# An encoder layer on one core: attention queues from a planner, output kept turned, next head's loads on GpSimd

## The reference

```
h = rms(x, g_pre_mix);  z = h @ w_in  -> q, k, v, forget logits, B, C, u
attn[t] = softmax_{s<=t}( q_t.k_s/8 + sum_{s<j<=t} logsigmoid(f_j + b_f) ) @ v     8 heads of 64
conv    = B * causal_conv3(C * u)                                                 512 channels
mix = concat(rms(attn, g_attn_out), rms(conv, g_conv_out)) @ w_o
x = x + rms(mix, g_post_mix)
x = x + rms(relu(rms(x, g_pre_mlp) @ w_up)^2 @ w_down, g_post_mlp)
```

## Time and profile before

| | us |
|---|---|
| median of 3 runs (2731.07 to 2736.04) | 2732.44 |
| the profiled execution, its own time | 2737.44 |
| its span, first to last instruction | 2735.8 |
| input projection, to the first score matmul | 621.9 |
| attention, to the first mixing product | 462.6 |
| mixing, to the MLP's block | 223.9 |
| MLP | 1427.4 |

### The profile page before, as it was taken

How to read it: one execution, slowest core, us unless ns; L and a number is a source line. 1 busy time by engine, 2 the same in 40 slices (tenths; PEclk the granted TensorE clock), 3 DMA queues, 4 the chain that set the end, 5 groups by cost and what they waited for, 6 DMA issues and landing times.

```text
span 2735.8 us, 41595 instructions
## 1 busy us (share of the span) xinstructions
PE 2664.9 (97%) x14966; PEld 2405.3 (88%) x14966; DVE 1515.6 (55%) x2603; ACT 1126.6 (41%) x2099; POOL 1300.7 (48%) x884
## 2 busy tenths in 40 slices
PE   8999999998999999999999999899999999999997
PEld 8999999897888888888889989889999988999996
DVE  5233344247888887765344344665556564556554
ACT  3201301107777877555333332534333344333433
POOL 3233334220101006553477776766556677566654
PEclk9999999999999999999999999999999999999999
DMA  6643534574565443568444546421211272212213
GB/s 199 199 123 110 175 108 142 189 199 103 124 150 122 100 102 117 167 183 244 143 168 163 196 169 225 170 74 64 77 61 61 85 277 96 73 61 66 72 61 108
DMA packets 294353, 364.26 MB, mean 133 GB/s; under 512 B 37576, under 2 KB 245392, under 8 KB 290128
## 3 DMA queue, kind: packets, MB, share of 16 engines
q1 hardware_dynamic: 257152, 316.15, 37.7%
q0 software_dynamic: 11808, 26.74, 3.1%
q10 hardware_dynamic: 25264, 19.66, 2.1%
HBM read 264.30 MB, written 97.94 MB: 132 GB/s over the span
## 4 chain that ended last, share of the span: by engine, by line
PE 46%; DVE 2%; POOL 1%; DMA 1%; issue 1%; ACT 0%; SPq 0%; DVEq 0%; POOLq 0%; ACTq 0%
PE dn_bank L3006 17%; PE up_bank L2982 15%; PE dn_bank L2962 7%; PE up_bank L2937 7%; DMA m_raw_up<-in_w_up 1%; DVE m_raw_up L2758 1%; POOL m_y L2517 1%; POOL m_w_up L2466 1%; DVE m_t L2758 0%; SPq L2342 0%; ACT m_junk L2659 0%; DVE m_y L2863 0%; DMA m_x<-scratch_x 0%; POOL m_u L2509 0%; DVE m_y L2817 0%
## 5 line engine op out<-in xcount | busy, mean ns | idle before, releaser
L3006 PE MATMUL dn_bank<-m_w_dn,m_u 128*128 128x512 f32 x2304 | 531.0, 391 | 5.4 <-ACT m_y L2692 4.3
L3006 PEld LDWEIGHTS dn_bank<-m_w_dn,m_u 128*128 128x128 f32 x2304 | 432.7, 188 | 96.0 <-ACT m_y L2692 4.0
L2982 PE MATMUL up_bank<-m_h,m_w_up 128*128 128x384 f32 x2688 | 476.1, 337 | 8.7 <-DVE m_stage L2772 4.5
L2982 PEld LDWEIGHTS up_bank<-m_h,m_w_up 128*128 128x128 f32 x2688 | 470.1, 189 | 12.7 <-issue 5.1
L2819 DVE TENSOR_TENSOR m_y<-dn_bank,m_y 128x1024 f32<-128x1024 f32 x168 | 205.7, 1224 | 270.4 <-PE dn_bank L3006 270.4
L508 POOL TENSOR_TENSOR w_lo<-w_raw,w_hi 128x1024 fp32r<-128x1024 f32 x72 | 176.0, 2448 | 342.3 <-DVE w_hi L722 342.3
L2509 POOL TENSOR_TENSOR m_u<-m_stage,m_u 128x384 fp32r<-128x384 f32 x128 | 141.5, 1128 | 281.7 <-ACT m_u L2648 281.7
L2466 POOL TENSOR_TENSOR m_w_up<-m_raw_up,m_w_up 128x512 fp32r<-128x512 f32 x128 | 192.2, 1521 | 65.2 <-ACT m_w_up L2616 65.2
L938 PE MATMUL proj<-ha_hi,w_hi 128*128 128x384 f32 (+1 forms) x640 | 212.1, 331 | 0.0
L1446 DVE TENSOR_TENSOR p_lo<-t_bank,p_hi 128x512 fp32r<-128x512 f32 (+1 forms) x336 | 197.9, 599 | 25.2 <-ACT p_hi L1393 24.6
L938 PE MATMUL proj<-ha_hi,w_lo 128*128 128x384 f32 (+1 forms) x640 | 210.0, 328 | 0.0
(11 more groups left out here) (304 smaller groups left out, 5674.4 us busy)
## 6 DMA issues: line engine op xcount, KB each, us to landing
m_raw_up<-in_w_up SPq DMA_DIRECT2D x48, 1024.0 KB, 5.4
m_raw_dn<-in_w_down SPq DMA_DIRECT2D x47, 1024.0 KB, 4.9
w_raw<-in_w_in SPq DMA_DIRECT2D x72, 512.0 KB, 4.1
scratch_h_pairs<-m_pieces POOLq DMA_DIRECT2D x12, 1792.0 KB, 8.2
m_h<-scratch_h_pairs SPq DMA_DIRECT2D x14, 1536.0 KB, 10.8
nck<-scratch_ncum SPq DMA_DIRECT2D x8, 1312.0 KB, 19.2
scratch_v_hl<-vhl SPq DMA_DIRECT2D x20, 512.0 KB, 2.7
q_hi<-scratch_q_hi SPq DMA_DIRECT2D x16, 528.0 KB, 7.3
```

Source lines behind the costliest of these rows:

```text
L2982: mm = pe.matmul(out, w_up[:, j, wp, k, :], hidden_rows(g, j, hp, k), start=(k == 0 and p == 0), stop=(k == KH - 1 and p == 2))
L3006: mm = pe.matmul(bank[:, cols], part, wd[:, wp, b, cols], start=(b == 0 and p == 0), stop=(b == 1 and p == len(passes) - 1))
```

## The change

- The looped order becomes one list of groups for all eight heads (attention_steps), in the order 0, EXTRA, 1, 2, 3. attention_order walks through it like a small planner: it has a cost and a latency for each step on PE, DVE and ACT, and appends to the engine's queue the step that can start first, by FIRST_CHOICE on a tie.
- N is gone. o_bank stays turned: ScalarE copies its lower and its upper 64 partitions to two places of o_t, GpSimd adds and scales them with 64 partitions and 512 columns, SP stores to attn_t (columns by rows). There are two o_bank.
- The scales are needed along columns now: VectorE makes a group's reciprocals at its first T, SP stores them to the scratch tensor rtotal and loads them back broadcast to 64 partitions.
- GpSimd issues the ten loads of head h+2 after it has closed group 3 of head h, and in the place of those of head 8 the eight of w_o. SP has the stores and the scales.
- g_attn_out and g_conv_out are multiplied into w_o by GpSimd, ahead of each split. The mixing loads attention rows turned from attn_t: its transposes and the multiplications by the gains are gone. Both squares and their sums are on GpSimd (sum_blocks), both rests too (rests), both high parts on ScalarE (firsts). A second matmul sums the attention's squares.

```diff
-S_BANKS, T_BANKS, O_BANKS = 3, 3, 1
-DELAY = {"act": {"M": 6, "T": 1, "O": 3, "N": 2}, "dve": {"M": 1, "T": 3}}
+S_BANKS, T_BANKS, O_BANKS = 3, 3, 2
 P_BUFS = 4
-A_BUFS = 5
+A_BUFS = 2
+GROUP_ORDER = (0, EXTRA, 1, 2, 3)
+SPLITS = {0: (5, 6), EXTRA: (4,), 1: (7, 0, 1), 2: (2, 3)}
+FIRST_CHOICE = {"pe": "TSV", "dve": "TS", "act": "TMO"}
...
+    def cost(engine, x):
+        if engine == "pe":
+            if x.kind == "S":
+                return 2 * (x.width / 2.4 + 13) + (107 if x.last else 0), 320
+            if x.kind == "T":
+                return 109 * (x.width // P), 260
+            return (2 * len(x.blocks) * 107 if x.group.extra else 2 * (x.width / 2.4 + 13)), 300
+        if engine == "dve":
+            return x.width / 0.96 + 67, 150
+        if x.kind == "O":
+            return 2 * (x.width / 1.2 + 150), 50
+        return x.width / 1.2 + (285 if x.kind == "M" else 125), 100
...
+    while True:
+        chosen = None
+        for engine, kinds in FIRST_CHOICE.items():
+            for rank, kind in enumerate(kinds):
+                n = taken[engine][kind]
+                if n < len(flat[kind]):
+                    x = flat[kind][n]
+                    start = max(free[engine], ready(engine, x))
+                    if start < math.inf and (chosen is None or start < chosen[0] or (start == chosen[0] and engine == chosen[1] and rank < chosen[2])):
+                        chosen = start, engine, rank, x
...
@@ sync @@
+            for q in groups:
+                store_scales(q)
+                load_scales(q)
+                if q is final[3]:
+                    sp.wait_ge(taken, S_BANKS + ALL_TAKEN)
+                    stored(final[0])
+                    stored(final[EXTRA])
                     front.load_first(sp)
+                if q.k:
+                    store(groups[q.k - 1])
...
@@ gpsimd @@
+            def fetch(head):
+                par = head % 2
+                pool.wait_ge(blank, 2)
+                if head >= 2:
+                    pool.wait_ge(used, P_BUFS + groups[GROUPS_OF * (head - 1) - 1].products[-1].at + 1)
+                if head == HEADS:
+                    front.load_weights(pool)
+                    return
+                load_queries_keys(pool, dr, head, q_hi[par], q_lo[par], k_hl[par], qk_fetched[par])
+                load_decay(pool, dr, head, nck[par], nck_fetched[par])
+                load_values(pool, dr, head, v_hl[par], v_fetched[par])
+
+            def close(q):
+                place, halves = att[0:HD, q.k % A_BUFS, 0:wide(q)], [o_t[0:HD, q.k % 2, i, 0:wide(q)] for i in range(2)]
+                pool.wait_ge(o_taken, O_BANKS + q.k + 1)
+                if q.k >= A_BUFS:
+                    pool.wait_ge(att_stored[q.k % A_BUFS], 16 * (q.k // A_BUFS))
+                pool.tensor_tensor(place, halves[0], halves[1], ALU.add).then_inc(added, 1)
+                pool.wait_ge(added, q.k + 1)
+                pool.wait_ge(scales_loaded[q.k % 2], 16 * (q.k // 2 + 1))
+                pool.tensor_tensor(place, place, scales[0:HD, q.k % 2, 0:wide(q)], ALU.mult).then_inc(att_done, 1)
+
+            fetch(1)
+            for q in groups:
+                if q is final[3]:
+                    pool.wait_ge(taken, S_BANKS + ALL_TAKEN)
                     front.set_ones(pool)
+                    front.sum_blocks(pool, 0, 0)
+                    front.rests(pool, 0, 0)
+                close(q)
+                if q.head == HEADS - 1 and q.g in SPLITS:
+                    for k in SPLITS[q.g]:
+                        front.split_weights(pool, k)
+                if q.g == GROUP_ORDER[-1] and q.head + 2 <= HEADS:
+                    fetch(q.head + 2)
...
@@ scalar @@
+                    act.wait_ge(used, P_BUFS + q.products[-1].at + 1)
+                    if q.k >= 2:
+                        act.wait_ge(added, q.k - 1)
+                    bank = o_bank[q.k % O_BANKS]
+                    act.activation(o_t[0:HD, q.k % 2, 0, 0:q.wide], bank[0:HD, 0:q.wide], ACT.Copy)
+                    act.activation(o_t[0:HD, q.k % 2, 1, 0:q.wide], bank[HD:P, 0:q.wide], ACT.Copy).then_inc(o_taken, 1)
...
@@ split_weights, load_first, sum_blocks, rests @@
+        pool.tensor_scalar(self.w_raw[:, k, :], self.w_raw[:, k, :], self.gains[:, k:k + 1], None, ALU.mult).then_inc(self.S["w_scaled"], 1)
...
+        sp.dma_start(self.a_in[:, 1, :, :], attn[:, :, 0:P]).then_inc(self.a_loaded[1], 16)
...
+            pool.tensor_tensor(q[:, n], rows[:, s], rows[:, s], ALU.mult).then_inc(S["squared"], 1)
...
+        pool.tensor_tensor(q[:, :, 0:2, :], q[:, :, 0:2, :], q[:, :, 2:4, :], ALU.add).then_inc(S["halves_summed"], 1)
...
+        pool.tensor_tensor(self.square_sums[:, :, :], q[:, :, 0, :], q[:, :, 1, :], ALU.add).then_inc(S["blocks_summed"], 1)
...
+        pool.tensor_tensor(self.a_lo[:, s], self.a_in[:, s], self.a_hi[:, s].bitcast(F32), ALU.subtract).then_inc(S["a_lo_done"], 1)
...
+        pool.tensor_tensor(self.c_lo[:, s], self.c_in[:, s], self.c_hi[:, s].bitcast(F32), ALU.subtract).then_inc(S["c_lo_done"], 1)
...
@@ mix_rows, tensor @@
-            def turn(t, s):
...
+                pe.matmul(q_bank[:, 0:1], square_sums[:, 0, :], ones[:, :], start=True, stop=True)
+                pe.matmul(q_bank[:, 1:2], square_sums[:, 1, :], ones[:, :], start=True, stop=True).then_inc(S["rows_summed"], 1)
```

More of the change, by code:

```diff
@@ new lines, in __init__, with attention_steps, step @@
+        self.blocks, self.cols, self.turn = blocks, cols, turn
+        self.first, self.last = first, last
+        self.maximum, self.last_score = None, None
+def attention_steps():
+    groups, count = [], dict.fromkeys("SMTVO", 0)
+    def step(kind, group, **more):
+        count[kind] += 1
+        return Step(kind, group, count[kind] - 1, **more)
+    for head in range(HEADS):
+        for g in GROUP_ORDER:
+            q = Group(len(groups), head, g)
+            same = [p for p in groups if p.set == q.set and not (q.extra and p.head == head)]
+            q.before = same[-1] if same else None
+            for tile in q.tiles:
+                if q.extra:
+                    pieces = [(0, PAST), (PAST, DEC)]
+                else:
+                    pieces = [(c, min(512, (tile + 1) * P - c)) for c in range(0, (tile + 1) * P, 512)]
+                for n, (col, width) in enumerate(pieces):
+                    q.scores.append(step("S", q, tile=tile, n=n, col=col, width=width, last=n == len(pieces) - 1))
+                q.maxima.append(step("M", q, tile=tile, n=len(pieces), width=pieces[-1][0] + pieces[-1][1]))
+                for x in q.scores[-len(pieces):]:
+                    x.maximum = q.maxima[-1]
+                q.maxima[-1].last_score = q.scores[-1]
+            if q.extra:
+                units = [(tuple(range(CB)), slice(0, CB * P)), ((CB,), slice(0, P))]
+            else:
+                units = [((j,), slice(max(0, j - 4 * g) * P, 512)) for j in range(4 * g + 4)]
+            for n, (blocks, cols) in enumerate(units):
+                edge = dict(first=n == 0, last=n == len(units) - 1)
+                t = step("T", q, blocks=blocks, cols=cols, width=cols.stop - cols.start, **edge)
+                q.turns.append(t)
+                q.products.append(step("V", q, blocks=blocks, cols=cols, width=cols.stop - cols.start, turn=t, **edge))
+            q.out = step("O", q, width=q.wide)
+            groups.append(q)
+    return groups
@@ L1406, in _ @@
[L1406 to L1415 removed]
+                    act.wait_ge(turned, 1 + x.at + 1)
+                    act.wait_ge(used, x.at + 1)
@@ L1417, in _ @@
+            for x in queues["act"]:
+                step(x)
         @block.vector
@@ L1942, in step @@
                     mix(t - 1, 1 - s)
-                if nxt and (not isinstance(t, int) or t >= 1):
-                    scale_rows(t + 1, 1 - s)
                 if is_split(t - 2) and t >= 2:
```

665 lines of the change are left out of this document (243 added, 422 removed).

## The result

The changed kernel took 2855.3 us (median of 4 runs, 2854.76 to 2860.55), the kernel before 2731.84 (4 runs, 2731.07 to 2736.04): a ratio of 1.0453, 95% interval 1.0435 to 1.0471. It is slower by 123 us; the forecast was 2710, and its range ended at 2740.

A forecast was written before the change was run, and what follows sets the result against it. PE, busy 97% of the span, was taken as the bound. Attention -32.2, GpSimd's last-head queue +14.8 and turned rows -5.3 gave -22.7, from 2732.4 to 2709.7 us; range 2688 to 2740, likeliest 2695 to 2725.

The forecast's parts named there:

- Reciprocals by way of HBM. Hidden: Attention: SP's store and broadcast load of each group's reciprocals would be hidden, as GpSimd multiplies only after the last product.
- my rivals: Three alternatives: GpSimd's queue not late, 2690 us (20 in 100); order regains nothing, 2729 (12); GpSimd held by loads, 2794 (13).
- the slower one: Attention: GpSimd held about 17 us per head while its loads drain, +84 us, total 2794; 13 in 100.
- Planned order, 52.7 us a head: Attention: fixed planned order regains more than half of 4.6 us lost per head; 57.3 to 52.7, -32.2 us for seven heads.
- PE's need, 50.8: Attention: PE's counted work per head without output transposes, 50.8 us, the bound if all waits were regained.
- Output transposes and o copies: Attention: seventeen output transposes per head go, 1.9 us, with their wait; ScalarE's load stays with two half-partition copies.
- Head loads on GpSimd, nothing: Attention: ten load issues per head move from SP to GpSimd, some 9.4 us, fitting with over 1 us spare; no cost.
- that rival's mechanism: GpSimd standing at its head loads because earlier ones had not drained, as SP's ninth load stood 17.75 us.
- GpSimd's queue in the last head, +14.8: Last head: GpSimd's added scaling and issues delay c_lo, mixing starts at 69.0 not 55.9, +13.1, plus 1.7 for the clock.
- my upper bound of 2.42: Last head: GpSimd's scaling of 1024 columns costs no more than the two-tile subtraction, 2.42 us; 1.72 was taken.
- Rows turned, -5.3: Mixing: four transposes per tile go, a second sum of squares comes, -4.9 us over 17 tiles, last output's transposes -0.4.

The follow-up runs named there:

- e7: Changed kernel with the four reciprocals of a partition stored side by side (128 pieces of 16 bytes, not 512 of 4), rows divided by other rows' sums: 2739.7 us.
- e1: Changed kernel without the reciprocals' store and load through HBM, multiplying by a constant tile, so rows are not divided by their sums: 2735.0 us, ratio 0.9991.
- e12: e9 with SP instead of GpSimd issuing the head loads, behind the store of a head's last group: 2723.7 us, ratio 0.9961.
- e5: e1 with mix_gains (32 bytes per partition) allocated behind the attention's tiles instead of ahead of most other tiles: 2718.5 us, ratio 0.9944.
- e9: Changed kernel with reciprocals stored in 16-byte pieces, read in strides to match rows, and mix_gains behind the attention's tiles; all computed: 2723.9 us, ratio 0.9961.

## Why the prediction was wrong

- **The step that failed: "Reciprocals by way of HBM. Hidden".** I had asked when the scales are needed (after the last product) and not how long the trip takes, nor what stands behind its wait on SP. There was no row for a store in 4-byte pieces, and instead of bounds I gave it nothing. It cost 116 us (e7, against the changed kernel) to 120 (e1). None of my rivals was this one: the slower one had its delay on GpSimd, by issues; the wait was on SP, by landings. The one clue was in the code: five waits for a landing per head, each ahead of the next store in one queue, and a head of 53 us allows 10 us each.
- **Planned order, 52.7 us a head:** 53.7 without the trip. The mechanism was right, and better than I said: nothing is lost. What was too low is PE's need, 50.8; a gapless head is 53.5 (321.26 busy us in six heads). Term: -25 instead of -32 for seven heads.
- **Output transposes and o copies:** gone without a trace, as said.
- **Head loads on GpSimd, nothing:** right without the trip. Ten issues took 6.2 us, not 9.4: 0.55 for most, 1.22 for the largest. GpSimd wasn't held either: the ninth load, on which SP stood 17.75 us, took 0.58 here, so that rival's mechanism didn't act, and e12 shows that with joined stores the move gained nothing. Nor did the rule that I had cited beside it (the Trainium skill, SBUF — State Buffer, SBUF: two separate sides): issues took 0.55 to 1.22 us in heads in which VectorE was busy 70% of the time, so no run here shows it; and the page's 3.1 us is what such a DMA takes, where I had read an issue.
- **GpSimd's queue in the last head, +14.8:** mechanism and place right. In e1 the wait was 26.3 us. The terms: scaling 2.85 us each and not 1.72, beyond my upper bound of 2.42 (+9.0); the eight issues 4.2 and not 7.5 (-3.3). I had bounded an operation with one input by one with two. The Trainium skill (GPSIMD Engine Reference, 3.1 Elementwise), by whose best figure I had 1.54 us, was further off than the rows; the cast's row was no neighbour. In the changed kernel the firsts on ScalarE waited 27.7 us for a_in as well, since SP's chain had also put off its loads.
- **Rows turned, -5.3:** a tile went from 12.50 to 12.30 us where the weights' tiles lie on 64 bytes (e5; I said from 12.54 to 12.25), 3 us in all. So of the 0.29 us that I took off a tile 0.20 came; why not the rest wasn't followed up. In the changed kernel and in e1 the place of mix_gains took this back: 12.49 again. And from the last tile to the end it is 1446.6 us in e1, 1439.1 before, 1433.1 in e5. That a new tile moves others was visible in the code; that it matters was in no row that I read. This is a second step that failed: a term that I hadn't in the sum at all, 12.8 to 16.5 us.
- **In sum:** without the trip (e1) the kernel is at 2735.0, the forecast was 2710. These 25 us are, as near as single profiles tell, 7 in the heads, 6 in GpSimd's queue and 12.8 to 16.5 by the place of mix_gains.

What stays open: why stores in 4-byte pieces are slow. The idle DMA engines in the windows above speak against their own work time, so the wait lies behind the last packet's start; whether in the memory or on the way to it no run here tells, nor from which size of piece on it goes away. And why a weights' tile off 64 bytes makes a product 6 ns longer, while the weight loads themselves show 187 to 188 ns in both. It can't be the only condition, since the 392 products of m_w_dn_even took 394 to 396 ns in all three kernels, before too, and those of the attention 394. That the MLP of e5 is 6 us shorter than before is explained in part at most: in the profile of before PE stood 4.3 us for ScalarE's m_y, in that of e5 it didn't.

## What to carry to other kernels

When a step goes through HBM and back, price the landing, not the issue, and multiply it by the times that one queue does it in a row; hidden means that the queue that waits has nothing else to do. Look at the size of the pieces that such a store is cut into. If a wait goes away and another of the same length takes its name, look for an engine without idle time, here SP's queue. And before you add a small tile, look which tiles it moves: put it last, as e5 did.

## What the runs showed of the hardware

- SP waited 11.5 us on the mean, up to 20.9, for a store of reciprocals in pieces of 4 bytes; with four stores of five in 128 pieces of 16 bytes 5.7. By kind, from SP's timeline: 512 pieces of 4 bytes 10.4, the 64 pieces of 4 bytes beside the head loads 16.3, 128 pieces of 16 bytes 4.3.
- The landing of a store in 4-byte pieces came 7.1 us (median) after the start of its last packet, with DMA engines idle; in 16-byte pieces 0.9. Stores of att beside them took 9.7 us to land, not 3.5.
- In the mixing and the MLP a product of 512 columns whose weights lie 32 bytes off a multiple of 64 took 395 ns, else 389 or 390; in 2752 products of the MLP and 816 of the mixing this was 12.8 to 16.5 us. Products with m_w_dn_even (394 to 396) and those of the attention (394) showed no such difference.
- GpSimd's multiplication of 128x1024 by a value per partition took 2.85 us, the subtraction of two tiles 2.40, the cast 1.04; ScalarE did the same scaling in 1.14.
- A GpSimd multiplication of 64x512 with one input in strides of 16 bytes took 1.55 us, with both dense 1.29 (e9, e1). The Trainium skill (SBUF — State Buffer, Specifications (TRN2)) says that SBUF is read by lines of 16 bytes and wants two uses of each for full speed; this stride uses each once, and the trace agrees that it costs, by a fifth; that it is the line, and not the pattern of two dimensions, isn't shown.
